# Splitting both weight pieces of the next job behind the first attention step of a turn

## The reference, cut to what matters

```python
def even_layer(x, ln, w_in, qkn, lam, subln, w_out, layer):
    h = rmsnorm(x, ln)
    aq, ak, av, az, bq, bk, bv, bz = split_cols(h @ w_in, EVEN_SPLITS_2)
    ...      # dilated attention on a, differential attention on b
    return x + mixed @ w_out

def odd_layer(x, ln, w_in, qkn, phi_pe, phi_w1, phi_w2, w_out):
    h = rmsnorm(x, ln)
    cq, ck, cv, cz, dq, dkc, dvc, dks, dvs, dkw, dvw, dz, dg = split_cols(h @ w_in, ODD_SPLITS)
    ...      # block attention on c; compressed, selected and windowed attention on d
    return x + mixed @ w_out
```

## Time and profile before

| | us |
|---|---|
| median of 3 runs | 1547.42 |
| lowest and highest | 1545.94, 1553.42 |
| the profiled execution | 1549.47 |
| its span, first to last instruction | 1547.6 |
| PE, DVE, ACT busy in the span | 1441.5, 1156.5, 847.2 |

### The profile page before, as it was taken

One profiled execution on the slowest core, in us unless ns is written; L12 is line 12 of the kernel. 1 busy time (PEld: TensorE's weight loads), 2 busy tenths in 40 slices (PEclk: granted clock), 3 DMA queues, 4 the chain that ended last, 5 costly groups with the idle time before them and its releaser, 6 DMA issues. The chain is left out here.

```text
span 1547.6 us, 23401 instructions
## 1 busy us (share of the span) xinstructions
PE 1441.5 (93%) x8807; PEld 1242.4 (80%) x8807; DVE 1156.5 (75%) x2067; ACT 847.2 (55%) x1612; POOL 0.2 (0%) x4
## 2 busy tenths in 40 slices
PE   3999998997988999989999899899999899989988
PEld 3878888996867888878888787688887788888766
DVE  6888878877678888788889856797657666656655
ACT  1545445563446454465445556564554766656763
POOL 0000000000000000000000000000000000000000
PEclk9999999998999999999999999999999899999999
DMA  9989885740036898559887333466555436527200
GB/s 370 343 307 343 307 262 186 238 149 1 1 113 228 301 317 308 199 177 327 321 284 266 113 108 130 150 230 230 193 190 184 130 95 233 139 82 243 85 1 28
DMA packets 197382, 306.16 MB, mean 198 GB/s; under 512 B 10551, under 2 KB 158998, under 8 KB 197270
## 3 DMA queue, kind: packets, MB, share of 16 engines
q1 hardware_dynamic: 196464, 304.40, 57.7%
q10 hardware_dynamic: 806, 0.26, 0.1%
HBM read 303.59 MB, written 1.05 MB: 197 GB/s over the span
## 5 line engine op out<-in xcount | busy, mean ns | idle before, releaser
L915 PE MATMUL bank<-u_hi_lo,w_hi 128*128 128x512 f32 x1344 | 472.6, 396 | 10.2 <-DVE arena L981 10.2
L914 PE MATMUL bank<-u_hi_lo,w_lo 128*128 128x256 f32 x1176 | 328.0, 279 | 0.0
L970 DVE TENSOR_TENSOR w_lo<-weight_ring,w_hi 128x1024 fp32r<-128x1024 f32 x264 | 308.0, 1219 | 17.8 <-ACT w_hi L940 17.0
L915 PEld LDWEIGHTS bank<-u_hi_lo,w_hi 128*128 128x128 f32 x1344 | 246.2, 188 | 62.5 <-DVE arena L981 14.4
L940 ACT CAST w_hi<-weight_ring 128x1024 fp32r<-128x1024 f32 x264 | 260.5, 1048 | 40.0 <-DMA weight_ring<-in_ffn_w_gate_dram 27.0
L914 PEld LDWEIGHTS bank<-u_hi_lo,w_lo 128*128 128x128 f32 x1176 | 221.7, 189 | 7.3
L837 PE MATMUL bank<-src_hi,wp_hi 128*128 128x256 f32 (+2 forms) x672 | 192.0, 301 | 1.4 <-ACT src_hi L434 1.2
L837 PE MATMUL bank<-src_hi,wp_lo 128*128 128x256 f32 (+2 forms) x672 | 180.0, 282 | 0.0
L837 PE MATMUL bank<-src_lo,wp_hi 128*128 128x256 f32 (+2 forms) x672 | 179.9, 283 | 0.0
L353 DVE SCALAR_TENSOR_TENSOR zT<-weight_ring,silu_c,zT 128x1024 f32<-128x1024 f32 x126 | 161.6, 1282 | 4.8 <-DMA weight_ring<-in_mod_w_dram 2.1
L2970 DVE TENSOR_TENSOR wp_lo<-weight_ring,wp_hi 128x1024 fp32r<-128x1024 f32 (+1 forms) x79 | 95.2, 1213 | 72.5 <-ACT wp_hi L2934 72.4
(11 more groups left out here) (382 smaller groups left out, 2316.0 us busy)
## 6 DMA issues: line engine op xcount, KB each, us to landing
weight_ring<-in_mod_w_dram SPq DMA_DIRECT2D x72, 1024.0 KB, 6.9
weight_ring<-in_ffn_w_gate_dram SPq DMA_DIRECT2D x44, 1024.0 KB, 6.1
weight_ring<-in_ffn_w_up_dram SPq DMA_DIRECT2D x44, 1024.0 KB, 5.4
weight_ring<-in_ffn_w_down_dram SPq DMA_DIRECT2D x44, 1024.0 KB, 8.2
weight_ring<-in_hyb_w_in_dram SPq DMA_DIRECT2D x16, 1024.0 KB, 8.2
weight_ring<-in_w_in_e_dram SPq DMA_DIRECT2D x16, 1024.0 KB, 7.7
weight_ring<-in_w_in_o_dram SPq DMA_DIRECT2D x13, 1024.0 KB, 6.0
weight_ring<-in_hyb_w_out_dram SPq DMA_DIRECT2D x4, 1024.0 KB, 4.9
```

The source lines that it names most:

```text
L914: nc.tensor.matmul(bank[:, 0:SEQ], w[1], u[:, 0:SEQ], start=False, stop=False, skip_group_check=True)
L915: last = nc.tensor.matmul(bank[:, :], w[0], u, start=kt == 0, stop=kt == KT - 1, skip_group_check=True)
L970: nc.vector.tensor_tensor(part_view(wl, n, part), raw, part_view(wh, n, part).bitcast(F32), ALU.subtract).then_inc(w_lo.sem, w_lo.up())
```

## The change

Both pieces of the next job are now split behind the first attention step of the turn, on ACT and on DVE. In a turn without a step they stand behind what is hung on the turn. No instruction is added or dropped, and PE's and SP's programs are the same. Line numbers behind the place fall by 2 to 4.

```diff
                 for j in range(1, n_jobs + 1):
-                    if j + 1 < n_jobs:
-                        split_hi(j + 1, slice(0, 1))
                     if j - 1 < n_proj:
...
                     for i in turns[:1]:
                         steps.act(act, i)
                     if j + 1 < n_jobs:
-                        split_hi(j + 1, slice(1, None))
+                        split_hi(j + 1)
...
                 for j in range(n_jobs):
                     for run in before_dve.get(j, ()):
                         run(dve)
-                    if j + 1 < n_jobs:
-                        split_lo(j + 1, slice(0, 1))
                     for run in at_dve.get(j, ()):
                         run(dve)
...
                         steps.dve(dve, i)
-                    if j + 1 < n_jobs and len(pieces[j + 1]) > 1:
-                        split_lo(j + 1, slice(1, None))
+                    if j + 1 < n_jobs:
+                        split_lo(j + 1)
```

## The result

The changed kernel takes 1561.72 us, the median of 6 runs (1555.37 to 1565.86). Timed beside it, the kernel before has a median of 1547.70 (6 runs, 1543.61 to 1553.42). The ratio is 1.0085, with a 95% interval of 1.0069 to 1.0101: 0.85% or 13.2 us slower (the two medians are 14.0 us apart). The forecast was 1553.6, with a range up to 1560.0. It had the direction right and half the size.

A forecast was written before the change was run, and what follows sets the result against it. PE, busy for 93% of the span, was taken to bound the kernel. The terms, 3.7 + 0.7 + 1.6 - 1.4 + 1.6 = +6.2 us, put the median at 1553.6 us, range 1549.0 to 1560.0.

The forecast's parts named there:

- Terms 1 and 2: Odd layer: PE waits 3.73 us for job 5's low part (+3.7); job 6 adds 1.5 less 0.8 (+0.7).
- Term 3: Odd layer, behind job 5's stall: PE's clock falls to half, +1.6 us, taken between 0 and 3.
- the rule quoted there: Trainium skill: leave no long pause between matmul bursts in mid-kernel, since the clock then falls back to half.
- Term 5: Even layer, turns 10, 12, 13 and 16: later splits make PE wait, +1.6 us, between 0 and 3.
- Term 4: Odd layer, jobs 12 to 16: steps start earlier without the split in front, -1.4 us, bounds 0 and 3 gained.
- the sign named for it: Odd layer, turns 12 to 15, profile after: no wait at the second step but one at the third.
- Rival (b): Whole kernel clearly slower: 10.6 us in all, 1558.0 us, chance 28%.
- its three pieces: Clock low for 6 us (+1.4), falling again at job 6 (+1.6), tight turns giving nothing back (+1.4).
- What bounds the kernel now: PE, busy 93% of the span; its waits read were for DVE scaling attention rows, 4.2 and 3.5 us.

The follow-up runs named there:

- experiment 3: Full change with unread TensorE products filling the pauses of turns 12 to 15, of job 5, or both: 1554.61, 1554.26 and 1553.02 us.
- all_but_turn4: Full change, but with the old order in the odd layer's turn 4, against the kernel before: 1550.83 us, ratio 1.0022.
- odd_tight: The change in the odd layer's turns from 11 on alone, against the kernel before: 1546.99 us, ratio 1.0014.

## Why the prediction was wrong, point by point

**Terms 1 and 2 (jobs 5 and 6, +3.7 and +0.7)** held: 3.62 us of wait where 3.73 was reckoned, 1.55 us before job 6, the 0.79 us wait gone. Without any fall the stretch is 4.65 us longer (29.71, in a trace with job 5's pause filled, against 25.06); the forecast had 4.4.

**Term 3 (the clock behind job 5, +1.6)** had the mechanism and about the size: one fall costs 1.5 us (31.20 - 29.71), the longer one 2.5 (32.19 - 29.71). It was treated as a thing that either happens or doesn't, though, when it happens in some executions of the same program and at different places: behind job 5 twice and near job 6 twice, in four traces. The reading in the prediction that by the rule quoted there the low clock would be certain here is not what the runs show: of seven traces with this pause unfilled, five have it.

**Term 5 (even layer, +1.6)** held: 1.7 us between the two openings (1.2 to 1.7 with them) in the traces of the full change, made of a wait of 1.0 us for L2859 (turn 10; 0.75 foreseen) and of 0.42 us for job 17's low part (0.6 foreseen).

**Term 4 (jobs 12 to 16, -1.4) is the step that failed.** What it said of the waits is what the traces show, down to the sign named for it: no wait at the second step, one at the third, and a stretch that without a fall is 0.9 us shorter from turn 7 on. But it added up waits and never asked what merging them does. Two pauses of 0.57 and 1.10 us in turn 13 became one of 2.05. Before, the clock stayed at 1.00 through these turns. Now it fell behind two or three of the pauses in three of four traces, and cost 3.2 to 5.7 us, 0.4 us for each us at half clock. The average over the four traces is 3.6 us, against -1.4 for the gain. The term's upper end was 0, where it should have been near +5. The earlier trace rows held the hint: there the clock had fallen near a pause of 2.20 us, hardly longer than those that this term creates, and the forecast priced that only for job 5's stall. The pause just before that one was shorter still, in the trace of before:

```profile
1356.46 1.06 PE L425 MATMUL bank<-tables_sb,zT 128*128 128x128 f32 x8 [1.66 <-DVE zT L756]
```


**The sum.** Fixed parts: 1.7 + 4.65 - 0.9 = 5.4 us, where the forecast had 4.6 without its clock term. The clock adds 2.0 us in A and 3.6 in the tight turns on average over the four traces, where the forecast had 1.6 for both. That makes 11.0 us, beside the 11.8 and 13.2 us that the two timings gave. The 1 to 2 us between are not assigned to a place; the draws of the clock differ by more from one execution to the next.

**Rival (b)** was right in part: a longer time at half clock behind job 5 (two traces), a fall near job 6 (two other traces). Its third condition, that the tight turns give nothing back, was too mild, since it never had them lose. Its 1558.0 us was the nearest of the cases, though no trace of the full change had both of its falls at once. The remark that it takes two of its three pieces to pass 7.7 us is a slip: 6.2 with the 1.6 at job 6 is already 7.8. The range ended at 1560.0, 1.7 us short of the median, because this case's own upper end had no clock in turns 12 to 15.

**What bounds the kernel now.** The prediction left out PE's largest waits in this part of the trace: 12.1 us in the openings of the two layers (L425). The change doesn't touch them, so nothing of the sum hangs on it.

## What to carry to other kernels

When two waits of TensorE merge into one, the sum of the waits need not be the whole price: look up what the clock did behind pauses of the new length in the same trace, and price it for every place that gets one. If it differs from trace to trace, compare stretches that hold the same matmuls, and read them by their granted clock. Before moving work ahead of or behind a step, find the point of the turn where the engine that does it already waits: here that was behind the third step, and it gave 6.7 us where the change as made lost 13.

## What was not expected of the hardware

The granted clock falls behind a pause of one and the same length in some executions and not in others. Behind the pauses of turns 12 to 15 (1.49, 2.05, 1.89 and 1.91 us, repeated to a tenth of a us; the last is 1.6 where the clock had fallen in turn 14 for 6.8 us) it fell in three of the four traces of the full change, in one of the three with only job 5 filled, in that of all_but_turn4, and not in that of odd_tight. With eight matmuls (1.21 us) inside each such pause it fell in neither of two traces. Four of the nine unfilled traces had no fall there either, so the stronger evidence for the fillers is the medians of experiment 3. In B, with PE busy for over 90% of it, 13.5 us at half clock cost 5.7 us.
